# Four edits to a hybrid mixer and mixture-of-experts layer: order of the pooling and branch steps, of w_out's loads, gates on expert rows, adding gathers

## What is computed

```python
def pool_mixer(u, w_pg, pool_scale):
    outs = []
    for g, w in enumerate(POOL_WINDOWS):
        ug = u[..., g * POOL_GROUP:(g + 1) * POOL_GROUP]
        outs.append(jnp.einsum('brlc,cd->brld', window_mean(ug, w) - ug, w_pg[g]))
    return jnp.concatenate(outs, axis=-1) * pool_scale
...
    pool = pool_mixer(p.reshape((b,) + grid + (D_POOL,)), w_pg, pool_scale).reshape(b, t, D_POOL)
    hg = hgrn2_readout(o2, og, hg_norm_w)
    m = jax.nn.sigmoid(gp) * (pool @ w_bp) + jax.nn.sigmoid(gh) * (hg @ w_bh)
    return m @ w_out
...
        xl = xl + mod_l[2] * yl
        hl2 = rmsnorm(xl, norm2_w[i]) * (1 + mod_l[4]) + mod_l[3]
        f = moe_ffn(hl2.reshape(-1, d), w_router, router_bias, w_e1[i], w_e3[i], w_e2[i])
        xl = xl + mod_l[5] * f.reshape(xl.shape)
    return rmsnorm(xl, final_norm_w)
```

## Time and profile before

| what | value |
|---|---|
| median of 3 runs | 2370.89 us (2370.41 to 2371.39) |
| the profiled execution | 2369.99 us |
| its span | 2368.3 us |
| mean granted TensorE clock | 0.969 of full |
| busy: PE / DVE / ACT / POOL | 92 / 65 / 42 / 22 % |
| PE's share of the chain that ended last | 24 % (DVE, DMA 1 % each) |

### The profile page before, as it was taken

The page is one execution under the profiler, slowest core; times in us unless marked ns, Lnnn a source line. Parts: engine busy times, 40 slices in busy tenths (PEclk is TensorE's granted clock), DMA queues, the critical chain, the costliest instruction groups (busy, mean ns, idle before and its releaser), DMA issues. The chain is left out here.

```text
span 2368.3 us, 33260 instructions
## 1 busy us (share of the span) xinstructions
PE 2190.2 (92%) x10804; PEld 1801.3 (76%) x10804; DVE 1550.6 (65%) x1916; ACT 987.6 (42%) x1199; POOL 523.8 (22%) x669
## 2 busy tenths in 40 slices
PE   4789999999999999899999999899789999999970
PEld 2569888888888886678777877688678888888860
DVE  3368555665566555666656664643768999999966
ACT  3234323233323323322222221332258888888862
POOL 0037434552545254111111111100000011001001
PEclk9899999999999999999999999899989999999995
DMA  8975552222222222677677765633589999999965
GB/s 334 364 232 158 154 178 83 82 80 82 78 86 80 82 73 80 200 228 241 209 221 228 241 210 197 222 129 134 190 334 394 419 415 419 421 417 416 420 249 213
DMA packets 332904, 532.31 MB, mean 225 GB/s; under 512 B 12416, under 2 KB 258704, under 8 KB 302896
## 3 DMA queue, kind: packets, MB, share of 16 engines
q1 hardware_dynamic: 299232, 392.92, 47.1%
q0 software_dynamic: 33616, 138.65, 16.2%
HBM read 494.79 MB, written 36.73 MB: 224 GB/s over the span
## 5 line engine op out<-in xcount | busy, mean ns | idle before, releaser
L1493 DVE TENSOR_TENSOR w_lo<-raw,w_hi 128x1024 fp32r<-128x1024 f32 x272 | 351.7, 1293 | 381.6 <-ACT w_hi L1105 380.5
L1105 ACT CAST w_hi<-raw 128x1024 fp32r<-128x1024 f32 x272 | 284.9, 1047 | 625.6 <-PE ps L671 287.2
L669 PE MATMUL ps<-hl_hi,w_hi 128*128 128x512 f32 x1280 | 508.5, 397 | 1.4 <-DVE hl_lo L1559 1.4
L671 PE MATMUL ps<-hl_hi,w_lo 128*128 128x512 f32 x1280 | 498.5, 389 | 0.0
L670 PE MATMUL ps<-hl_lo,w_hi 128*128 128x512 f32 x1280 | 498.3, 389 | 0.0
L1917 DVE TENSOR_TENSOR e_lo<-e_raw,e_hi 128x1024 fp32r<-128x1024 f32 x384 | 456.1, 1222 | 50.7 <-ACT e_hi L1359 37.5
L1359 ACT CAST e_hi<-e_raw 128x1024 fp32r<-128x1024 f32 x384 | 399.5, 1059 | 87.7 <-PE ps L988 87.7
L671 PEld LDWEIGHTS ps<-hl_hi,w_lo 128*128 128x128 f32 x1280 | 240.3, 188 | 50.7
L669 PEld LDWEIGHTS ps<-hl_hi,w_hi 128*128 128x128 f32 x1280 | 240.6, 188 | 50.3 <-issue 3.2
L670 PEld LDWEIGHTS ps<-hl_lo,w_hi 128*128 128x128 f32 x1280 | 240.7, 188 | 49.0 <-issue 1.7
L986 PE MATMUL ps<-e_hi,xe_hi 128*128 128x512 f32 x512 | 203.3, 397 | 4.3 <-DVE e_lo L1917 2.9
(11 more groups left out here) (342 smaller groups left out, 3604.7 us busy)
## 6 DMA issues: line engine op xcount, KB each, us to landing
e_raw<-in_w_e SPq DMA_DIRECT2D x192, 1024.0 KB, 9.8
raw<-in_w_in SPq DMA_DIRECT2D x208, 512.0 KB, 3.7
ada<-in_w_ada POOLq DMA_DIRECT2D x64, 1024.0 KB, 5.8
ada_ring<-in_w_ada SPq DMA_DIRECT2D x32, 1024.0 KB, 11.5
raw<-in_w_out SPq DMA_DIRECT2D x32, 512.0 KB, 3.7
block_outputs<-y_sb POOLq DMA_DIRECT2D x32, 512.0 KB, 6.5
raw<-in_w_branch_pool SPq DMA_DIRECT2D x16, 512.0 KB, 3.9
raw<-in_w_branch_hgrn SPq DMA_DIRECT2D x16, 512.0 KB, 3.9
```

The costliest lines, as they stand in the source:

```text
L669: mm(dst, hi, rhs_hi[:, k, :], start=(k == 0), stop=False)
L671: last = mm(dst, lo, rhs_hi[:, k, :], start=False, stop=(k == KT - 1))
L1105: act_e.copy(w_hi[:, hslot, :], raw[:, slot, :]).then_inc(hi_done, 1)
L1493: tt(w_lo[:, hslot, :], raw[:, slot, :], w_hi[:, hslot, :].bitcast(F32), ALU.subtract).then_inc(split_done, 1)
```

## The change

**Pool mixer.** `w_pg` is loaded by SP, right behind both directions' last states (`s_rdy`), into its own room, in place of POOL after the last head. PE uses four banks in place of two. `poolT` is now `delta` itself: ACT writes two tiles once the pair's inputs have been read. ACT alternates pool outputs, the cast of hg and that of poolT by pairs. DVE scales seven of the eight hg tiles inside the last `lat_scan` call. In the merge the hgrn branch comes first (`part_h`), the pool branch second.

**w_out.** SP loads units 0 and 1 ahead of everything, then two `m_sb` loads, units 2 and 3, and the rest. `merged_lo(0)` stands between the last two products on DVE; PE waits for these at its third and fourth token tile.

**Gates.** 16 more 24-column matmuls make `gate_tab`, the gate of each row of each expert's block, from high and low parts of the gates; `y_copy` is scaled by it. Filler behind the table: 12 matmuls in place of 32.

**Tail.** The number of extra blocks is read before the last store, and the loop stands between that store's issue and the wait for it. Tiles 0 and 1: two gathers and an addition as before. Tiles 2 and 3: y0 is gathered, and y1 is gathered onto it by a DMA with `compute_op` add. ACT no longer scales.

The diff, cut to its core:

```diff
-        w_pg = Room(nc, base, 114, 122).new("w_pg", [P, 4, 2, 256], F32)
+        w_pg = Room(nc, base, 194, 202).new("w_pg", [P, 4, 2, 256], F32)
...
-        poolT = Room(nc, base, 146, 162).new("poolT", [P, HEADS, SEQ], F32)
+        poolT = delta
...
-                for u, w in ((4, w_bp_d), (5, w_bh_d)):
+                for u, w in ((4, w_bh_d), (5, w_bp_d)):
...
+            load_branches(0)
+            sp.wait_ge(s_rdy[0], HEADS)
+            sp.wait_ge(s_rdy[1], HEADS)
+            sp.dma_start(w_pg[:], w_pg_d).then_inc(consts_in, 16)
             with sp.Fori(0, KT - 1) as j:
-                load_branches(j)
                 for u in range(4):
                     load_gates(j + 1, u, j * 6 + (6 + u))
-            load_branches(KT - 1)
-            sp.wait_ge(units_done, 2 + S_W - 2)
...
-            for n in range(KT // 2 - 1):
+            load_out(0, 0, 2)
+            sp.wait_ge(units_done, 2 + S_W - 2)
+            for n in range(2):
                 load_merged(n, 16 + 32 * (KT - 1))
-            load_out(0, 0, 4)
+            load_out(0, 2, 4)
+            for n in range(2, KT // 2 - 1):
+                load_merged(n, 16 + 32 * (KT - 1))
             load_merged(KT // 2 - 1, 32 * KT)
             load_out(0, 4, 8)
...
             pe.wait_ge(pool_rdy, HEADS)
-            pe.wait_ge(coef_in, 16 * (HEADS + 1))
+            pe.wait_ge(consts_in, 96)
             pe.wait_ge(lv_sel, HEADS * 8)
             pe.wait_ge(gate_rdy, HEADS)
             pe.wait_ge(p_ev, HEADS)
             for t in range(HEADS):
                 g, half = t // 2, t % 2
-                if t >= 2:
-                    pe.wait_ge(pg_ev, t - 1)
+                if t >= 4:
+                    pe.wait_ge(pg_ev, t - 3)
                 for k in range(2):
-                    last = mm(bank((BF, BB)[t % 2]), w_pg[:, g, k, half * P:(half + 1) * P], delta[:, 2 * g + k, :],
-                              start=(k == 0), stop=(k == 1))
+                    last = mm(bank((BF, BB, BD, TR)[t % 4]), w_pg[:, g, k, half * P:(half + 1) * P],
+                              delta[:, 2 * g + k, :], start=(k == 0), stop=(k == 1))
                 last.then_inc(pg_mm, 1)
             def branches(j):
                 pe.wait_ge(m_rdy, j + 1)
-                for u, a_hi, a_lo, b, pieces in ((4, poolT_hi, poolT_lo, BF, 4), (5, hg_hi, hg_lo, BB, 8)):
-                    pe.wait_ge(h_split, H_PIECES + pieces)
+                for u, a_hi, a_lo, b, p_sem, p_count in ((4, hg_hi, hg_lo, BF, h_split, H_PIECES + 7),
+                                                         (5, poolT_hi, poolT_lo, BB, h_split, H_PIECES + 8)):
+                    pe.wait_ge(p_sem, p_count)
...
-            pe.wait_ge(m_rdy, KT + 1)
...
+                        if cb == 0 and u == 0 and t == 2:
+                            pe.wait_ge(ph_rdy, KT + 1)
+                        if cb == 0 and u == 0 and t == 3:
+                            pe.wait_ge(m_rdy, KT + 1)
...
-            keep_busy(8)
-            pe.wait_ge(table_rdy, 1)
-            keep_busy(24)
+            pe.wait_ge(gate_mm, 1)
+            for z in range(2):
+                for n in range(2 * NTOK):
+                    last = mm(ps[:, 2, 0:NBLK + 1], slot_1[:, n, :], block_gate[:, z, n, :],
+                              start=(z == 0 and n == 0), stop=(z == 1 and n == 2 * NTOK - 1))
+            last.then_inc(gate_mm, 1)
+            keep_busy(12)
...
-            for t in range(HEADS):
-                act_e.wait_ge(pg_mm, t + 1)
-                if t == HEADS - 1:
+            def pool_out(t):
+                act_e.wait_ge(pg_mm, 2 * (t // 2) + 2)
+                activate(poolT[:, t, :], bank((BF, BB, BD, TR)[t % 4]), ACT.Copy,
+                         scale=vecT[:, V_PS + t:V_PS + t + 1]).then_inc(pg_ev, 1)
+            def pool_hi(n):
+                act_e.wait_ge(pg_ev, 2 * n + 2)
+                act_e.copy(poolT_hi[:, 2 * n:2 * n + 2, :], poolT[:, 2 * n:2 * n + 2, :]).then_inc(h_hi, 1)
+            def hg_hi_piece(n):
+                act_e.wait_ge(hgw_rdy, 2 * n + 2)
+                act_e.copy(hg_hi[:, 2 * n:2 * n + 2, :], hg[:, 2 * n:2 * n + 2, :]).then_inc(h_hi, 1)
+            pool_out(0)
+            pool_out(1)
+            for n in range(4):
+                if n < 3:
+                    pool_out(2 * n + 2)
+                    pool_out(2 * n + 3)
+                hg_hi_piece(n)
+                if n == 0:
                     act_e.wait_ge(hg_rdy, HEADS + 1)
-                activate(poolT[:, t, :], bank((BF, BB)[t % 2]), ACT.Copy, scale=vecT[:, V_PS + t:V_PS + t + 1]
-                         ).then_inc(pg_ev, 1)
-            act_e.wait_ge(pg_ev, HEADS)
-            for n in range(8):
-                if n == 4:
-                    act_e.wait_ge(hgw_rdy, 1)
-                dst, src = ((poolT_hi, poolT), (hg_hi, hg))[n // 4]
-                k = 2 * (n % 4)
-                act_e.copy(dst[:, k:k + 2, :], src[:, k:k + 2, :]).then_inc(h_hi, 1)
+                pool_hi(n)
...
-                    act_e.copy(y_sb[:, part * 512:(part + 1) * 512], bank(2 + part)).then_inc(y_ev, 1)
+                    activate(y_sb[:, part * 512:(part + 1) * 512], bank(2 + part), ACT.Copy, scale=gate_of(b)
+                             ).then_inc(y_ev, 1)
...
-                act_e.wait_ge(y_in[i], 32)
-                activate(y0[:, i, :], y0[:, i, :], ACT.Copy, scale=gate_w[:, 0, i:i + 1]).then_inc(y0_rdy, 1)
-            for i in range(NTOK):
                 act_e.wait_ge(f_sum, i + 1)
                 own.wait()
                 own.did(activate(f_junk[:], o_sb[:, i, :], ACT.Square, accum_out=stat2[:, 0, i:i + 1]))
...
+            def weigh(hd):
+                ts(hg[:, hd, :], hg[:, hd, :], vecT[:, V_HG + hd:V_HG + hd + 1], None, ALU.mult).then_inc(hgw_rdy, 1)
             def lat_scan(h, main, lag):
                 hd = h - 1
                 for u in range(H_U if main else 11):
+                    if not main and u == 4:
+                        dve.wait_ge(hg_rdy, HEADS)
+                        for t in range(HEADS - 1):
+                            weigh(t)
...
-            for hd in range(HEADS):
-                last = ts(hg[:, hd, :], hg[:, hd, :], vecT[:, V_HG + hd:V_HG + hd + 1], None, ALU.mult)
-            last.then_inc(hgw_rdy, 1)
+            weigh(HEADS - 1)
             for n in range(8):
                 dve.wait_ge(h_hi, H_PIECES + n + 1)
-                dst, src, hi_ = ((poolT_lo, poolT, poolT_hi), (hg_lo, hg, hg_hi))[n // 4]
-                k = 2 * (n % 4)
+                dst, src, hi_ = ((hg_lo, hg, hg_hi), (poolT_lo, poolT, poolT_hi))[n % 2]
+                k = 2 * (n // 2)
                 tt(dst[:, k:k + 2, :], src[:, k:k + 2, :], hi_[:, k:k + 2, :].bitcast(F32), ALU.subtract
                    ).then_inc(h_split, 1)
...
-                        tt(part_p[:], bank(BF), sig_gp[:], ALU.mult).then_inc(pp_rdy, 1)
+                        tt(part_h[:], bank(BF), sig_gh[:], ALU.mult).then_inc(ph_rdy, 1)
+                        if last:
+                            merged_lo(0)
...
+            own.did(dve.tensor_copy(gate_hi[:], gate_w[:]))
+            own.wait()
+            own.did(tt(gate_lo[:], gate_w[:], gate_hi[:].bitcast(F32), ALU.subtract))
+            own.wait()
+            own.did(dve.tensor_copy(block_gate[:, :, :, NBLK], SM(15)[:, 0:4 * NTOK].rearrange("p (z n) -> p z n", z=2)))
+            for z, part in enumerate((gate_hi, gate_lo)):
+                last = tt(block_gate[:, z, :, 0:NBLK], block_tok[:], part[:].bitcast(F32).rearrange("p z t -> p (z t)")
+                          .unsqueeze(2).to_broadcast([P, 2 * NTOK, NBLK]), ALU.mult)
+                if z == 0:
+                    own.did(last)
+            own.wait()
+            last.then_inc(gate_mm, 1)
...
-                dve.wait_ge(y0_rdy, i + 1)
-                step(stt(out=o, in0=y1[:, i, :], scalar=gate_w[:, 1, i:i + 1], in1=y0[:, i, :], op0=ALU.mult,
-                         op1=ALU.add))
-                step(tt(o, o, m5_row[:], ALU.mult))
+                if i < 2:
+                    dve.wait_ge(y_in[i], 32)
+                    step(tt(o, y0[:, i, :], y1[:, i, :], ALU.add))
+                    step(tt(o, o, m5_row[:], ALU.mult))
+                else:
+                    dve.wait_ge(y_in[i], 16)
+                    step(tt(o, y0[:, i, :], m5_row[:], ALU.mult))
...
-            pool.dma_start(w_pg[:], w_pg_d).then_inc(coef_in, 16)
-            pool.wait_ge(pg_mm, HEADS)
...
-            store(E - 1)
-            pool.wait_ge(y_out, 16 * (2 * E + NTOK))
             pool.wait_ge(xe_in, 16 * (E + 1))
             n_extra = pool.value_load(route_i[0:1, 7:8], min_val=0, max_val=NXTRA)
+            store(E - 1)
...
-                for z, dst in ((0, y0), (1, y1)):
-                    pool.indirect_dma_start(out=dst[:, i, :], out_offset=None, in_=y_d,
-                                            in_offset=bass.IndirectOffsetOnAxis(ap=dest_i[:, z, i:i + 1], axis=0)
```

(14 more changed lines are left out.)

62 lines of the change are left out of this document (36 added, 26 removed).

## The result

The changed kernel took 2341.06 us in the median of 4 runs (2339.93 to 2344.24), the one before 2371.14 beside it: a ratio of 0.9871, interval 0.9859 to 0.9883, 30.1 us less. Forecast were 2337.5 (2332 to 2348) and 33.4 less.

What follows compares the result with a forecast made beforehand. PE was busy 2190.2 of 2368.3 us, so only its standstills, half-clock stretches and the tail could move the end. Terms −7.3 − 14.1 + 2.0 − 14.0 = −33.4 from 2369.99 gave 2336.6, as a median 2337.5 (2332 to 2348).

Steps and rivals of the forecast that it cites:

- A: Pool mixer: earlier w_pg load, four banks and reordered casts let PE go on at 949.75 instead of 957.01, −7.3 us.
- B: Merge to w_out: earlier units and fewer row loads ahead close PE's 11.79 us hole and its low clock, −14.1 us.
- the −2.4 of the forecast: First to last w_out matmul: 12 matmuls no longer at the low clock behind the hole, 2.4 us less.
- three waits on PE: At w_out: merged_lo(0), m_row's bank and unit 1 were each forecast ready before PE wants them.
- C: Router: gate matmuls, fillers at the low clock and scaled copies were to cost +2.0 us (0 to +3.5).
- 0.35 per expert, hidden but for the last: Expert copies: ACT's scaling by the gate adds 0.35 us per expert, exposed only at the last store.
- D: Tail: earlier gathers, no ACT scaling, fewer DVE additions and a closed DVE hole, −14.0 us (−9 to −14.5).
- the prediction's case of double the moving time: Tail: adding gathers at 4.95 us each land at 2331.2 and 2336.1, still in time for DVE.
- the prediction's own list of signs: Trace checks; wrong if DVE waits for row 2 or 3, w_out's hole stays, or the 580 us expert stretch changes.
- The first rival: Tail: adding gathers cost three to four times a plain one, row 3 2 to 7 us late, 2343.5; chance 0.13.
- The second: Pool mixer and w_out: holes don't close, another wait ends last, the 0.50 clock stays, 2345.5 us; chance 0.12.
- The slower rival: Tail: the adding gather moves in small pieces, about 2382 us at 256 bytes, 2352 at 512; chance 0.03.

## Why the prediction was right, and where it was off

The direction, the four places and the main mechanism at each were right; 30.1 us came for 33.4. In the two traces the stretches of the change sum to −27.6, and the changed kernel's is its longest execution, so the fit of the medians flatters the sum a little. By its own steps:

- **A, −7.3, came −4.1** (−6.0 to −6.4 in the eight kernels without fillers there that kept the clock before the pool matmuls). The load's place (3.8 in its experiment), the pairs and the branch order did what was said. Two terms were mis-sized: w_pg was put at 5.0 us from issue to landing and took 6.1 (5.5 to 6.1 over the kernels that load it from SP), and the 32 matmuls, "at full clock", were to take 13.8. They take 13.97 at the full clock, but in the profiled run, with 1.4 us of standing ahead, they ran low at first and took 15.67.
- **B, −14.1, came −12.0.** The hole closed wholly; undoing the load order brought 9.4 back, undoing the waits 3.0 and a low clock. The step that failed is "m_lo of the other pairs is one cast and one subtraction per 6 us of PE, as before". DVE has the modulation steps between them, and the last of these waited for its load. That load took 5.4 us to land in the kernel before, and 5.7 and 5.9 in the two experiments where PE stood before w_out (9.26 and 2.85 us); in the changed kernel it took 11.0, and the w_out units issued around it 11.9 and 12.5. Without the hole the loads stand closer together; which of them holds it up no run separates. With the step moved behind them the stretch took 184.42 us, the −2.4 of the forecast. I asked what is late next for three waits on PE, and not for the queue of DVE.
- **C, +2.0, came +2.6 to the transposes.** Of this 1.0 is the low clock at the routing matmuls, ahead of the slot matrix, where no code differs; behind it the stretch grew by 1.6 (11.94 to 13.57). The low clock for the fillers was the right choice. Not foreseen was what the fillers gave: the start of the first expert at the full clock, where the kernel before ran low to 1730 (from the first transpose to the last standstill 3.0 us less). And "0.35 per expert, hidden but for the last" was wrong: it lies on the path once more before the last expert's second product, 0.46 us, with 1.6 of clock behind it. Together −0.9 in the expert stretch, which the prediction held nothing should touch.
- **D, −14.0, came −13.2.** Gathers 4.2 sooner (3.4), DVE 1.8 sooner behind them (2.1), ACT's hole gone, 4.6 of additions gone. The term that failed is the adding gather's 6.00 us as a plain one: a plain one at that time takes 7.1, with the add 10.4. Even the prediction's case of double the moving time had it at 8.6 us, and in time by 0.6. DVE wanted the row at 2318.98 and had it at 2320.34. By the prediction's own list of signs this wait, for row 2, says that the step was wrong; it cost 1.4 us of the 14.

The first rival was half of what happened: the gather was dear enough for DVE to wait, 1.4 us, at double its moving price and not at three to four times. The second did not come at A and B as I had it, but its clock did, at A. The slower rival fell: the adding gather moves at 215 GB/s.

From the last w_out matmul to the slot matrix all kernels take either 30.6 us, as the one before, or 31.1 to 31.7, though their code is the same there. The traces tell which: the eight longer ones are the eight whose routing matmuls ran low. What stays open is why the clock falls there in some and not in others, behind the same 1.47 us; no run was made for it. Nor for the start, which is up to 2.7 us apart from run to run.

## What to carry to other kernels

When a hole is closed, what was hidden in it comes forward, and the loads behind it stand closer together: go through the queue of each engine in the stretch behind it, with the landing time of each load, not only through the waits of the engine that stood. Look at the granted clock behind every standstill, too: before the pool matmuls, before the branches and at the last expert it cost 1.5 to 2.7 us each. At the last two fillers gave it back without delaying anything; at the first the clock held in eight kernels without them. An addition put into a gather takes the DVE time away at half the transfer rate, so it wants the gather issued early.

## What the runs showed that I had not expected

- The clock's fall goes with little: behind a standstill of 1.20 us or less before the pool matmuls it was at 1.00 in eight kernels, behind 1.38 or more it was not in four; at the last expert 2.97 and 3.42 were the two sides, without an exception in thirteen kernels. At w_out it fell behind 2.85 us. And at the routing matmuls one and the same 1.47 us had both outcomes, eight to six. So no one length decides, and each place is read by its own rows.
- Twelve fillers at the low clock (5.47 us) were as good as six or better, though six made the stretch 1.9 us shorter: 0.3 us worse in one execution of the changed kernel and 1.5 better in the other, since the products behind them then began at the full clock.
- A plain gather cost POOL 0.94 to 0.99 us to issue before DVE and ACT had rows to work on, and 2.0 to 2.4 while they worked. That their work is the reason is not shown.
